# Trainium2, two transformer blocks in one launch: the SiLU of the SSM's first eight channel blocks inside its sixth convolution unit, and the last convolution unit ahead of the SSM input's transposes

## The chip, the cores and the metric

The kernel runs on one core of a Trainium2 chip. The core has TensorE (PE, matrix products and transposes into PSUM), VectorE (DVE), ScalarE (ACT), GpSimd (POOL) and SyncE (SP, which here issues the weight transfers). Each engine runs its own instruction list in order, and the lists are tied together by counting semaphores. The metric is the device time of one launch in microseconds, lower being better.

## The reference, cut to what matters

The launch computes two transformer blocks for 256 tokens of width 1024 in fp32. The change lies in the first block's token mixer, and there in the state-space mixer (SSM):

```python
h = rms_norm(x, pre_mix_norm)
proj = h @ w_in                      # z, xbc, dt_raw, sb_qkv, nsa_q, nsa_kv, nsa_gate, merge_gate
xbc = silu(causal_dwconv(xbc, conv_w, conv_b))   # 2048 channels, 4 taps over time
xs, bm, cm = split(xbc, [1024, 1536])            # xs: SSM input; bm, cm: 4 groups x 128
# ssd_chunked: needs xs with the tokens on rows (times dt), and cm @ bm products
```

Beside the SSM, the same mixer holds a stick-breaking attention ("sb": products of q and k, a log-sigmoid, a reverse cumulative sum, an exponential, products with v) and a sparse attention ("kk", "kv", "vv", "nq"). The rest (gates, feed-forward networks, the second block) is not touched.

## The kernel before

**Units.** All the large weights come as a stream of 128 units of 128 x 2048 fp32 numbers (1 MB). The order is the list `UNITS`: sbq, sbk, sbv (two each, numbers 0 to 5), xbc 0 to 7 (numbers 6 to 13), kk (14), kv (15), vv (16), nq (two), z (four), and so on. SP loads a unit into one of three slots of `w_raw`, as soon as both halves of the unit three places before have been made. fp32 weights are used as a sum of two numbers that PE takes at its faster rate: ACT writes `w_hi` (a rounded copy, function `split` at L1130) and DVE writes `w_lo`, the difference (L1583). ACT may overwrite `w_hi` of a slot only when PE has finished the unit that used it (semaphore `unit_done`). The helper `ahead(name)`, on both engines, makes these halves up to two units beyond the named one, and does nothing when they are made already. For each unit PE multiplies the 256 tokens by the 256 output channels, for two halves of the columns and eight steps of 128 input channels, with three products each (`run_unit`: L466, L468, L469; 48 products), into one of three PSUM banks `pj`. DVE reads that bank out (`channel_major`, L1596), after which the bank is free (`pj_read`).

**Convolution.** A unit xbc i holds channel blocks 2i (even) and 2i+1 (odd). DVE's `conv_out(i)` copies the product to a buffer `xc` (two of them, taken in turn), and then calls `ahead`. ACT's `conv_first(i)` writes the first tap of both blocks (L1223), and one product for POOL (`conv_tap0`, L1231), for which it first waits until POOL has finished the odd block of the unit before (`conv_odd`, one shared buffer). DVE's `conv_taps(i)` adds three taps to the even block (L1599, in unit 7 to both blocks), and POOL's `conv_odd(i)` adds them to the odd block (L403, L406, L400). Then ACT's `silu(q)` treats blocks 4q to 4q+3 in one instruction (L1264). `silu(0)` and `silu(1)` cover the SSM input xs, `silu(2)` and `silu(3)` what becomes bm and cm.

**Order by hand.** Each engine's order is written out. PE: xbc 5, `sb_later(1)` (L636 to L639), xbc 6, a wait for two SiLUs (`xbc_silu` at 2), 16 transposes of the SSM input into PSUM regions S and T (L505), xbc 7, `sb_apply(1)` (L604, L605; needs DVE's `sb_mask(1)`), kk, kv, the "cb" products (L714, L718; need `xbc_silu` at 4), vv, `seg(0)` (L729; needs DVE to have read cb), and so on. ACT: `conv_first(5)`, `sb_exp(1)` (L1253), `silu(0)`, `silu(1)`, `conv_first(6)`, four copies of the transposed input (L1287), `silu(2)`, `conv_first(7)`, `sb_hi(1)` (L1258; needs `sb_apply(1)`), weights of vv, `silu(3)`. DVE: `conv(5)`, `sb_sum(1)`, `sb_mask(1)`, `gate_decay(0)`, `conv(6)`, `conv(7)`, `sb_lo(1)`, the two products xdt, and the read-outs of kk and kv.

ACT holds one set of function tables at a time. Exp and Silu are in different sets; Copy and Identity run with either (the trace shows no load ahead of them).

Of the kernel before, what the change touches and what calls it, by code (L numbers as in the profile page):

```python
# [130 lines left out]
def program(nc, stream, params, consts, cmpw, gains, x_in, out):  # L131
    ctx = ExitStack()
    with ctx:
        sems = {}

        def S(name):

            if name not in sems:
                sems[name] = ctx.enter_context(nc.semaphore(name))
            return sems[name]  # L140
# [29 lines left out]
        def V(kib, *dims):  # L170

            n = int(np.prod(dims))
            o = int(kib * 256)
            ap = area[:, o:o + n]
            if len(dims) == 1:
                return ap
            names = "abcd"[:len(dims)]
            return ap.rearrange(f"p ({' '.join(names)}) -> p {' '.join(names)}",
                                **dict(zip(names[1:], dims[1:])))
# [35 lines left out]
        xbc = V(36, 16, T)  # L215
        xc = [V(52, 2, T), V(54, 2, T)]
# [4 lines left out]
        kk, cm, vv = V(52, 2, T), V(54, 2, T), V(56, 2, T)  # L221
# [77 lines left out]
        def written(ins, region):  # L299
            ins.then_inc(S(f"{region}_written"), 1)  # L300
# [151 lines left out]
        def _(pe):  # L452
            def unit_ready(u):
                pe.wait_ge(S("w_hi_done"), u + 1)
                pe.wait_ge(S("w_lo_done"), u + 1)

            def bank_free(b, n):

                if isinstance(n, int) and n == 0:
                    return  # L460
                pe.wait_ge(S(f"pj_read{b}"), n)
# [11 lines left out]
            def unit_b(slot, b, koff=0, gate=None):  # L473

                for nb in range(2):
                    for k in range(KC):
                        if gate and nb == 0:
                            gate(k)
                        c = k * 256 + nb * P
                        mm = three(pj[b][:, nb * T:(nb + 1) * T], w_hi[:, slot, c:c + P], w_lo[:, slot, c:c + P],  # L480
                                   a_hi[:, koff + k, :], a_lo[:, koff + k, :], k == 0, k == KC - 1)
                mm.then_inc(S("unit_done"), 1)

            def unit_a(slot, b):

                for tb in range(2):
                    for k in range(KC):
                        c = k * 256
                        mm = three(pj[b][:, tb * 256:(tb + 1) * 256], w_hi[:, slot, c:c + 256],
                                   w_lo[:, slot, c:c + 256], a_hi[:, k, tb * P:(tb + 1) * P],  # L490
                                   a_lo[:, k, tb * P:(tb + 1) * P], k == 0, k == KC - 1, weights_left=False)
                mm.then_inc(S("unit_done"), 1)

            def run_unit(name, gate=None):
                u = UIDX[name]
                b, n = BANK[name]
                unit_ready(u)
                bank_free(b, n)
                if name[0] in ("sbv", "vv", "z", "dv", "fv"):
                    unit_a(u % SLOTS, b)  # L500
                else:
                    unit_b(u % SLOTS, b, 8 if name[0] == "wo2" else 0, gate)
# [188 lines left out]
            run_unit(("xbc", 5))  # L691
            sb_later(1)
            run_unit(("xbc", 6))

            pe.wait_ge(S("xbc_silu"), 2)
            claim(pe, "S", "xs")
# [6 lines left out]
                if q == 1:  # L703
                    written(mm, "S")
            written(mm, "T")
            run_unit(("xbc", 7))
            sb_apply(1)
            run_unit(("kk", 0))
            run_unit(("kv", 0))
            claim(pe, "T", "cb")  # L710
            claim(pe, "S", "cb")
# [151 lines left out]
            for n in range(8):  # L863
                name = ("br", n)
# [256 lines left out]
        def _(act):  # L1121
# [70 lines left out]
            for q in range(4):  # L1192
# [4 lines left out]
                for k in (2 * q, 2 * q + 1):  # L1197
                    act.activation(a_hi[:, k, :], pa[:, q, (k % 2) * T:(k % 2 + 1) * T], ACT.Copy,
                                   scale=g_mix1[:, k:k + 1]).then_inc(S("opnd_hi"), 1)
# [14 lines left out]
            for i in range(2):  # L1214
                token_major(("sbv", i), sbv[:, :, i * 256:(i + 1) * 256])

            def conv_first(i):

                ahead(("xbc", i))
                await_value(act, ("xbc", i))  # L1220
                for m in range(2):
                    blk = 2 * i + m
                    act.activation(xbc[:, blk, :], xc[i % 2][:, m, :], ACT.Identity,  # L1223
                                   bias=prm_("cb")[:, blk:blk + 1], scale=prm_("cw")[:, 48 + blk:49 + blk])\
                       .then_inc(S("conv_tap3"), 1)

                if i == 7:
                    return
                if i:
                    act.wait_ge(S("conv_odd"), i)  # L1230
                act.activation(conv_tap0, xc[i % 2][:, 1, :], ACT.Copy, scale=prm_("cw")[:, blk:blk + 1])\  # L1231
                   .then_inc(S("tap3_product"), 1)
# [18 lines left out]
            def sb_exp(p):  # L1251
                await_read(act, "T", f"sb{p}")
                act.activation(sb_w[p], sb_ls[p], ACT.Exp).then_inc(S("sb_exp_ready"), 1)  # L1253
# [7 lines left out]
            def silu(q):  # L1261
                act.wait_ge(S("conv_even"), 2 * (q + 1))
                act.wait_ge(S("conv_odd"), min(2 * (q + 1), 7))
                act.activation(xbc[:, 4 * q:4 * q + 4, :], xbc[:, 4 * q:4 * q + 4, :], ACT.Silu)\  # L1264
                   .then_inc(S("xbc_silu"), 1)
# [10 lines left out]
            conv_first(3)  # L1276
            conv_first(4)
            sb_hi(0)
            conv_first(5)
            sb_exp(1)  # L1280
            silu(0)
            silu(1)
            conv_first(6)
            for q in range(4):
                if q % 2 == 0:
                    await_psum(act, "ST"[q // 2], "xs")
# [4 lines left out]
                else:  # L1291
                    ins.then_inc(S("xs_half"), 1)
            silu(2)
            conv_first(7)
            sb_hi(1)
            ahead(("kk", 0))
            silu(3)
            act.activation(gate, small40[:, :, 16:40], ACT.Tanh, scale=0.5).then_inc(S("gate_tanh"), 1)
            ahead(("kv", 0))
            await_value(act, ("kv", 0))  # L1300
# [275 lines left out]
        def _(dve):  # L1576
# [11 lines left out]
            def ahead(name_or_u):  # L1588
                u = UIDX[name_or_u] if isinstance(name_or_u, tuple) else name_or_u
                while ahead_of[0] <= min(u + 2, N_UNITS - 1):  # L1590
                    split(ahead_of[0])
                    ahead_of[0] += 1
                return u
# [9 lines left out]

            rbc2 = rbc[:, :].unsqueeze(1).to_broadcast([P, 2, T])

            def channel_major(name, dst, scale=None):

                b, _n = BANK[name]
                dve.wait_ge(S("unit_done"), UIDX[name] + 1)
                ins = tt(dst, two(pj[b]), rbc2, ALU.mult) if scale is None \  # L1610
                    else stt(dst, two(pj[b]), scale, rbc2, ALU.mult, ALU.mult)
                ins.then_inc(S(f"pj_read{b}"), 1)
                ahead(name)

            def operand_lo(j, gname, k):
                g = prm_(gname) if j else g_mix1
# [102 lines left out]
            def conv_out(i):  # L1719

                if i >= 2:
                    dve.wait_ge(S("conv_tap3"), 2 * (i - 1))
                    dve.wait_ge(S("conv_odd"), i - 1)
                channel_major(("xbc", i), xc[i % 2])

            def conv_taps(i):

                await_value(dve, ("xbc", i))
                dve.wait_ge(S("conv_tap3"), 2 * i + 1)
                if i == 0:  # L1730
                    dve.wait_ge(S("prm_loaded"), 16)
                for s_ in (1, 2, 3):
                    for m in range(2 if i == 7 else 1):
                        blk = 2 * i + m
                        c = (3 - s_) * 16 + blk
                        if m:
                            dve.wait_ge(S("conv_tap3"), 2 * i + 2)
                        ins = stt(xbc[:, blk, s_:T], xc[i % 2][:, m, 0:T - s_], prm_("cw")[:, c:c + 1],
                                  xbc[:, blk, s_:T], ALU.mult, ALU.add)
                        if s_ < 3:  # L1740
                            V_.did(ins)
                    if s_ == 3:
                        ins.then_inc(S("conv_even"), 1)
                    else:
                        V_.sync()

            def conv(i):
                conv_out(i)
                conv_taps(i)
# [16 lines left out]
            def sb_sum(p):  # L1766
                await_psum(dve, "T", f"sb{p}")
                read(tt(sb_ls[p], sb_ls[p], pt[:, :, 0:384], ALU.add), "T")

            def sb_mask(p):  # L1770
                dve.wait_ge(S("sb_exp_ready"), p + 1)
                tt(outer_blocks(sb_w[p]), outer_blocks(sb_w[p]), sb_diag, ALU.mult).then_inc(S("sb_w_ready"), 1)
# [9 lines left out]
            def gate_decay(g):  # L1782

                tt(gdt, gt.unsqueeze(1).unsqueeze(1).to_broadcast([P, 2, 4, P]),
                   dta[:, :, 4 * g:4 * g + 4].unsqueeze(3).to_broadcast([P, 2, 4, P]), ALU.mult)\
                    .then_inc(S("gdt_ready"), 1)
# [24 lines left out]
            sb_lo(0)  # L1811
            conv(5)
            sb_sum(1)
            sb_mask(1)
            gate_decay(0)
            conv(6)
            conv(7)
            sb_lo(1)

            dve.wait_ge(S("xs_half"), 2)  # L1820
# [553 lines left out]
```

## Time and profile before

| | before |
|---|---|
| median of 3 runs | 909.22 us (903.97 to 910.04) |
| the profiled execution | 908.93 us |
| its span, first to last instruction | 907.1 us |
| outside the span | 1.8 us |
| PE busy | 868.4 us, 96% |
| DVE, ACT, POOL busy | 66%, 51%, 7% |
| mean granted clock of PE | 0.989 |

The profile is of one execution. Spans and durations are in microseconds from the first instruction. "Busy" of PE says that matrix products were in flight, not that they ran at the full rate, so an idle stretch is loss for certain and a busy one may hold loss too. The waits behind an idle stretch are inferred from semaphores, and the one named is the one that came last.

### The profile page before, as it was taken

The numbers are of one execution on the slowest core, as the hardware profiler recorded it, in microseconds if no ns is written. First come the engines' busy times: TensorE is split into PE (matmuls) and PEld (weight loads), VectorE is DVE, ScalarE is ACT, GpSimd is POOL, SyncE is SP. The second block draws the span as 40 slices with busy tenths as digits, with TensorE's granted clock in tenths as the row PEclk, the third lists the DMA queues.
The fourth block names the chain that finished last, engine by engine and source line by source line (L and its number), as shares of the span: only waits on it lengthen the run. The fifth ranks groups of instructions, "written<-read, shape, count | busy, mean of one in ns | idle before, by whom it ended". The sixth has DMA issues, their size and how long they took to land.

```text
span 907.1 us, 15574 instructions
## 1 busy us (share of the span) xinstructions
PE 868.4 (96%) x6246; PEld 805.4 (89%) x6246; DVE 594.3 (66%) x779; ACT 459.5 (51%) x648; POOL 64.7 (7%) x68
## 2 busy tenths in 40 slices
PE   6999799999999999999999999889998999999997
PEld 6999799999988998898999998789885899999995
DVE  4548785626776578678776776876454676555554
ACT  5456743337656444466554555565454463333332
POOL 0026700000000132000000000000000000000000
PEclk9999899999999999999999999999999999999999
DMA  9533352252423345555555555344313446555531
GB/s 341 217 133 140 115 211 94 93 165 79 164 96 137 124 180 197 191 181 186 187 185 185 186 186 186 108 171 141 139 47 116 150 153 222 190 190 186 185 139 47
DMA packets 22168, 143.83 MB, mean 159 GB/s; under 512 B 2928, under 2 KB 3188, under 8 KB 5728
## 3 DMA queue, kind: packets, MB, share of 16 engines
q1 hardware_dynamic: 20304, 138.30, 42.5%
q0 software_dynamic: 1808, 4.73, 1.5%
q8 instruction: 42, 0.69, 0.3%
q14 instruction: 14, 0.11, 0.0%
HBM read 141.96 MB, written 1.84 MB: 159 GB/s over the span
## 4 chain that ended last, share of the span: by engine, by line
PE 82%; DVE 7%; ACT 6%; issue 3%; POOL 2%; DMA 1%; SPq 0%; POOLq 0%; ACTq 0%; DVEq 0%
PE pj L466 16%; PE pj L469 13%; PE pj L468 13%; PE pa L891 6%; PE pa L892 6%; PE pa L893 6%; PE pj L471 2%; PE pj L470 2%; DVE w_lo L1583 2%; PE pa L505 2%; ACT w_hi L1130 1%; PE pj L569 1%; DVE area L1596 1%; ACT area L1374 1%; PE pj L575 1%
## 5 line engine op out<-in xcount | busy, mean ns | idle before, releaser
L1583 DVE TENSOR_TENSOR w_lo<-w_raw,w_hi 128x2048 fp32r<-128x2048 f32 x127 | 294.8, 2323 | 82.1 <-ACT w_hi L1130 81.9
L466 PE MATMUL pj<-a_hi,w_hi 128*128 128x256 f32 x1168 | 335.3, 287 | 0.6 <-issue 0.6
L469 PE MATMUL pj<-a_hi,w_lo 128*128 128x256 f32 x1168 | 332.5, 285 | 0.0
L468 PE MATMUL pj<-a_lo,w_hi 128*128 128x256 f32 x1168 | 332.4, 285 | 0.0
L1130 ACT ACTIVATE w_hi<-w_raw 128x2048 fp32r<-128x2048 f32 x127 | 241.9, 1907 | 56.2 <-PE pa L893 41.4
L466 PEld LDWEIGHTS pj<-a_hi,w_hi 128*128 128x128 f32 x1168 | 226.1, 194 | 5.5 <-issue 4.6
L468 PEld LDWEIGHTS pj<-a_lo,w_hi 128*128 128x128 f32 x1168 | 226.2, 194 | 0.8
L469 PEld LDWEIGHTS pj<-a_hi,w_lo 128*128 128x128 f32 x1168 | 226.0, 193 | 0.0
L891 PE MATMUL pa<-w_hi,a_hi 128*128 128x512 f32 x280 | 109.5, 391 | 4.2 <-issue 4.2
L892 PE MATMUL pa<-w_lo,a_hi 128*128 128x512 f32 x280 | 109.2, 390 | 0.0
L893 PE MATMUL pa<-w_hi,a_lo 128*128 128x512 f32 x280 | 108.9, 389 | 0.0
L1596 DVE TENSOR_TENSOR area<-pj,rbc 128x512 f32<-128x512 f32 x66 | 45.3, 688 | 76.2 <-PE pj L469 75.9
L891 PEld LDWEIGHTS pa<-w_hi,a_hi 128*128 128x128 f32 x280 | 52.7, 188 | 15.1 <-issue 4.8
L893 PEld LDWEIGHTS pa<-w_hi,a_lo 128*128 128x128 f32 x280 | 52.6, 188 | 11.1
L892 PEld LDWEIGHTS pa<-w_lo,a_hi 128*128 128x128 f32 x280 | 52.7, 188 | 9.9
L1599 DVE SCALAR_TENSOR_TENSOR area<-area,prm 128x255 f32<-128x255 f32 (+2 forms) x115 | 52.6, 507 | 2.9 <-ACT area L1223 1.4
L1417 ACT ACTIVATE area<-area,prm 128x256 f32<-128x256 f32 x44 | 24.0, 595 | 54.0 <-DVE area L1596 54.0
L466 PE MATMUL pj<-w_hi,a_hi 128*128 128x256 f32 x176 | 50.5, 287 | 0.0
L471 PE MATMUL pj<-w_hi,a_lo 128*128 128x256 f32 x176 | 49.8, 283 | 0.0
L470 PE MATMUL pj<-w_lo,a_hi 128*128 128x256 f32 x176 | 49.8, 283 | 0.0
L1552 ACT ACTIVATE a_hi<-area 128x512 fp32r<-128x512 f32 x16 | 10.1, 632 | 73.8 <-DVE area L1599 73.8
L1374 ACT ACTIVATE area<-area,tiny 128x128 f32<-128x128 f32 (+1 forms) x64 | 28.4, 444 | 29.4 <-DVE tiny L1953 29.4
(254 smaller groups left out, 1053.2 us busy)
## 6 DMA issues: line engine op xcount, KB each, us to landing
w_raw<-stream SPq DMA_DIRECT2D x127, 1024.0 KB, 4.8
area<-gains POOLq DMA_DIRECT2D x4, 512.0 KB, 4.2
cst<-consts SPq DMA_DIRECT2D x1, 1093.0 KB, 13.4
x_tok<-x_in SPq DMA_DIRECT2D x2, 512.0 KB, 5.0
w_raw<-stream SPq DMA_DIRECT2D x4, 256.0 KB, 6.9
area<-cmpw POOLq DMA_DIRECT2D x1, 1024.0 KB, 5.5
out<-x_tok SPq DMA_DIRECT2D x4, 256.0 KB, 2.0
t_wide<-t_rows POOLq DMA_DIRECT2D x1, 768.0 KB, 13.4
```

Source lines behind the costliest of these rows:

```text
L466: pe.matmul(out_, a[0], a[1], start=first, stop=False)
L468: pe.matmul(out_, wh, al, start=False, stop=False)
L469: return pe.matmul(out_, wl, ah, start=False, stop=last)
L470: pe.matmul(out_, ah, wl, start=False, stop=False)
L471: return pe.matmul(out_, al, wh, start=False, stop=last)
L891: pe.matmul(o_, a_hi[:, chunk + kc, rows], w_hi[:, slot, c:c + 512], start=first, stop=False)
L892: pe.matmul(o_, a_hi[:, chunk + kc, rows], w_lo[:, slot, c:c + 512], start=False, stop=False)
L893: return pe.matmul(o_, a_lo[:, chunk + kc, rows], w_hi[:, slot, c:c + 512], start=False, stop=last)
L1130: act.activation(w_hi[:, slot, :], w_raw[:, slot, :], ACT.Copy).then_inc(S("w_hi_done"), 1)
L1583: dve.tensor_tensor(w_lo[:, slot, :], w_raw[:, slot, :], w_hi[:, slot, :].bitcast(F32), ALU.subtract)\
L1596: return dve.tensor_tensor(o_, a, b, op)
L1599: return dve.scalar_tensor_tensor(out=o_, in0=a, scalar=s_, in1=b, op0=op0, op1=op1)
```

## The change

PE runs xbc 7 straight after xbc 6, then waits for the two SiLUs, then transposes; kk now comes ahead of `sb_apply(1)`. ACT gets an argument `between` for `conv_first`, which runs after the first taps and before the wait for POOL. Inside `conv_first(5)` this makes `w_hi` of kk (unit 14) and runs `silu(0)` and `silu(1)`. Inside `conv_first(6)` it runs `sb_exp(1)` and makes `w_hi` of kv (unit 15). `conv_first(7)` comes ahead of the copies of the transposes, and `silu(3)` follows `silu(2)`. DVE reads xbc 6 out ahead of `gate_decay(0)`, reads xbc 7 out ahead of `sb_mask(1)`, and makes `w_lo` of kv only after that (`split_next`). No work is added or taken away, except that the order of Exp and Silu on ACT is another.

```diff
--- before.py
+++ after.py
@@ -691,6 +691,7 @@
             run_unit(("xbc", 5))
             sb_later(1)
             run_unit(("xbc", 6))
+            run_unit(("xbc", 7))
 
             pe.wait_ge(S("xbc_silu"), 2)
             claim(pe, "S", "xs")
@@ -703,9 +704,8 @@
                 if q == 1:
                     written(mm, "S")
             written(mm, "T")
-            run_unit(("xbc", 7))
+            run_unit(("kk", 0))
             sb_apply(1)
-            run_unit(("kk", 0))
             run_unit(("kv", 0))
             claim(pe, "T", "cb")
             claim(pe, "S", "cb")
@@ -1214,7 +1214,7 @@
             for i in range(2):
                 token_major(("sbv", i), sbv[:, :, i * 256:(i + 1) * 256])
 
-            def conv_first(i):
+            def conv_first(i, between=lambda: None):
 
                 ahead(("xbc", i))
                 await_value(act, ("xbc", i))
@@ -1226,6 +1226,7 @@
 
                 if i == 7:
                     return
+                between()
                 if i:
                     act.wait_ge(S("conv_odd"), i)
                 act.activation(conv_tap0, xc[i % 2][:, 1, :], ACT.Copy, scale=prm_("cw")[:, blk:blk + 1])\
@@ -1276,11 +1277,21 @@
             conv_first(3)
             conv_first(4)
             sb_hi(0)
-            conv_first(5)
-            sb_exp(1)
-            silu(0)
-            silu(1)
-            conv_first(6)
+
+            def early_silu():
+
+                ahead(("xbc", 6))
+                silu(0)
+                silu(1)
+
+            def last_weights():
+
+                sb_exp(1)
+                ahead(("xbc", 7))
+
+            conv_first(5, early_silu)
+            conv_first(6, last_weights)
+            conv_first(7)
             for q in range(4):
                 if q % 2 == 0:
                     await_psum(act, "ST"[q // 2], "xs")
@@ -1291,10 +1302,9 @@
                 else:
                     ins.then_inc(S("xs_half"), 1)
             silu(2)
-            conv_first(7)
+            silu(3)
             sb_hi(1)
             ahead(("kk", 0))
-            silu(3)
             act.activation(gate, small40[:, :, 16:40], ACT.Tanh, scale=0.5).then_inc(S("gate_tanh"), 1)
             ahead(("kv", 0))
             await_value(act, ("kv", 0))
@@ -1603,14 +1613,15 @@
 
             rbc2 = rbc[:, :].unsqueeze(1).to_broadcast([P, 2, T])
 
-            def channel_major(name, dst, scale=None):
+            def channel_major(name, dst, scale=None, split_next=True):
 
                 b, _n = BANK[name]
                 dve.wait_ge(S("unit_done"), UIDX[name] + 1)
                 ins = tt(dst, two(pj[b]), rbc2, ALU.mult) if scale is None \
                     else stt(dst, two(pj[b]), scale, rbc2, ALU.mult, ALU.mult)
                 ins.then_inc(S(f"pj_read{b}"), 1)
-                ahead(name)
+                if split_next:
+                    ahead(name)
 
             def operand_lo(j, gname, k):
                 g = prm_(gname) if j else g_mix1
@@ -1721,7 +1732,7 @@
                 if i >= 2:
                     dve.wait_ge(S("conv_tap3"), 2 * (i - 1))
                     dve.wait_ge(S("conv_odd"), i - 1)
-                channel_major(("xbc", i), xc[i % 2])
+                channel_major(("xbc", i), xc[i % 2], split_next=(i < 7))
 
             def conv_taps(i):
 
@@ -1811,10 +1822,13 @@
             sb_lo(0)
             conv(5)
             sb_sum(1)
+            conv_out(6)
+            gate_decay(0)
+            conv_taps(6)
+            conv_out(7)
             sb_mask(1)
-            gate_decay(0)
-            conv(6)
-            conv(7)
+            ahead(("xbc", 7))
+            conv_taps(7)
             sb_lo(1)
 
             dve.wait_ge(S("xs_half"), 2)
```

## Rows read from the trace of the kernel before

**Rows 1.** The page's section 1 (busy time) and section 6 (weight loads).

```profile
PE 868.4 (96%) x6246; PEld 805.4 (89%) x6246; DVE 594.3 (66%) x779; ACT 459.5 (51%) x648; POOL 64.7 (7%) x68
...
w_raw<-stream SPq DMA_DIRECT2D x127, 1024.0 KB, 4.8
```

**Rows 2.** Timeline of PE: start, length, line, tiles, count, idle before it.

```profile
106.33 3.47 PE L505 MATMUL pa<-cst,area 128*128 128x128 f32 x16 [6.19 <-ACT area L1264]
109.55 0.36 PE L466 MATMUL pj<-a_hi,w_hi 128*128 128x256 f32 x1
...
115.39 0.59 PE L604 MATMUL po<-area 128*128 128x256 f32 x2
...
128.21 1.89 PE L714 MATMUL pa<-area 128*128 128x256 f32 x8
...
130.75 0.36 PE L466 MATMUL pj<-w_hi,a_hi 128*128 128x256 f32 x1
...
224.00 1.91 PE L505 MATMUL pa<-cst,area 128*128 128x128 f32 x16
```

**Rows 3.** Chain of work that ended last, before the transposes: start, length, what.

```profile
99.57 0.70 POOL area L400
...
100.30 0.51 ACT area L1231
```

**Rows 4.** Timeline of ACT: columns as in Rows 2.

```profile
96.56 1.08 ACT L1223 ACTIVATE area<-area,prm 128x256 f32<-128x256 f32 x2
...
102.98 1.28 ACT L1264 ACT_TABLE_LOAD   x1
104.27 2.00 ACT L1264 ACTIVATE area<-area 128x1024 f32<-128x1024 f32 x2
106.18 1.90 ACT L1130 ACTIVATE w_hi<-w_raw 128x2048 fp32r<-128x2048 f32 x1
...
109.37 2.02 ACT L1287 ACTIVATE area<-pa 128x512 f32<-128x512 f32 x4
111.28 1.06 ACT L1264 ACTIVATE area<-area 128x1024 f32<-128x1024 f32 x1
...
117.41 0.64 ACT L1258 ACTIVATE a_hi<-po 128x256 fp32r<-128x256 f32 x2
```

**Rows 5.** Timeline of DVE: columns as in Rows 2.

```profile
96.70 2.29 DVE L1583 TENSOR_TENSOR w_lo<-w_raw,w_hi 128x2048 fp32r<-128x2048 f32 x1 [0.27 <-ACT w_hi L1130]
98.91 2.30 DVE L1599 SCALAR_TENSOR_TENSOR area<-area,prm 128x255 f32<-128x255 f32 x3
101.13 0.94 DVE L1596 TENSOR_TENSOR area<-area,pa 128x768 f32<-128x768 f32 x1
102.99 0.69 DVE L1596 TENSOR_TENSOR area<-area,cst 128x512 f32<-128x512 f32 x1 [0.92 <-ACT area L1253]
103.60 1.66 DVE L1596 TENSOR_TENSOR area<-cst,tiny 128x1024 f32<-128x1024 f32 x1
105.18 0.68 DVE L1596 TENSOR_TENSOR area<-pj,rbc 128x512 f32<-128x512 f32 x1
108.11 2.29 DVE L1583 TENSOR_TENSOR w_lo<-w_raw,w_hi 128x2048 fp32r<-128x2048 f32 x1 [2.25 <-ACT w_hi L1130]
...
118.50 2.69 DVE L1599 SCALAR_TENSOR_TENSOR area<-area,prm 128x255 f32<-128x255 f32 x6
...
121.71 2.35 DVE L1596 TENSOR_TENSOR area<-area,tiny 128x1024 f32<-128x1024 f32 x2
```

**Rows 6.** Timeline of POOL: columns as in Rows 2.

```profile
91.06 2.72 POOL L400 TENSOR_TENSOR area<-area 128x253 f32<-128x253 f32 x1
```

**Rows 7.** Windows: length; busy PE, PEld, DVE, ACT, POOL; then granted clock.

```profile
103.00:104.00 1.00, 0.00 (x0) 0.00 (x0) 1.00 (x2) 1.00 (x1) 0.92 (x2) 0.50 0.41 164
...
110.00:111.00 1.00, 1.00 (x11) 1.00 (x10) 1.00 (x2) 1.00 (x3) 1.00 (x1) 1.00 0.00 0
230.00:231.00 1.00, 1.00 (x7) 1.00 (x7) 1.00 (x1) 1.00 (x2) 0.00 (x0) 0.50 0.08 16
```

## Prediction, written before the changed kernel ran

> **What bounds the kernel now.** I read the page first: PE is busy for 868.4 of 907.1 us, every other engine for at most two thirds [rows 1]. So the kernel ends when PE ends, and an edit is worth the PE time that it frees. Next, the waits of PE and its timeline in the first mixer. Between 60 and 180 us PE stands still once: for 6.19 us, ahead of the 16 transposes at 106.33, until an ACT instruction of L1264, which is SiLU [rows 2]. Xbc 6 was thus over at 106.33 - 6.19 = 100.14. Then the chain of waits, backwards from there: POOL's last add of conv_odd(4) ends at 100.27, ACT's L1231 had waited for it [rows 3], and behind that, on ACT's list, stand sb_exp(1), a table load and the two SiLUs, over at 106.27 [rows 4]. But the SiLUs need none of these. They need the even blocks of units 0 to 3, which DVE had done before its taps of unit 5 at 98.91 [rows 5], and conv_odd(3), over at 91.06 + 2.72 = 93.78 [rows 6]. The stall is one of order on ACT.
>
> Last, the windows, with PE's granted clock. In the idle stretch it is at 0.50, which is the level of 1.2 GHz, and at 110 it is back at 1.00, 2.4 GHz [rows 7]. So the transposes ran at half clock: 3.47 us, where the 16 transposes of the same shape at 224.00 took 1.91 [rows 2]. The stall costs 1.56 us more than its own length.
>
> **What the change takes away.** PE keeps its instructions: from 106.33 to 128.21, where the cb products start, it does transposes, xbc 7, sb_apply(1), kk and kv, without a wait, 21.88 us [rows 2]. In the new order the same work starts at 100.14 with xbc 7. Its weights are there: the `w_lo` ready at 96.70 + 2.29 = 98.99 is the one of unit 13 [rows 5]. Xbc 7 takes 115.39 - 109.55 = 5.84 us [rows 2], so the transposes are due at 105.98. If nothing holds them, PE has not stood still and they run at full clock: 21.88 - 1.56 = 20.32, cb starts at 120.46, and the gain is 6.19 + 1.56 = 7.75 us.
>
> **Does every wait on the way hold?** I follow the three other engines in their new order, with durations of the rows. These overlap their successors by some 0.08 us (98.91 + 2.30 is 101.21, the next starts at 101.13 [rows 5]), so the sums err towards late; hand-overs between engines, below 0.1 us each (106.27 to 106.33), go the other way.
>
> ACT: first taps of unit 5 end at 97.64. `w_hi` of kk, 1.90, to 99.54 (the slot was freed when PE ended xbc 5, which comes before xbc 6 and `sb_later`). Silu load 1.28, two SiLUs 2.00: 102.82 [rows 4]. The transposes want them at 105.98, margin 3.2. Then L1231, 0.51 [rows 3], to 103.33; first taps of unit 6, 1.08, to 104.41; Exp with its load. Those two took from 100.30 + 0.51 = 100.81 to 102.98 [rows 3, 4], 2.17: to 106.58. `w_hi` of kv, 1.90, to 108.48; L1231 to 109.0.
>
> DVE: from sb_sum(1) at 101.13, 0.94; read-out of xbc 6, 0.68; `w_lo` of kk, 2.29: 105.04 (kk starts on PE at 105.98 + 3.22 - 1.56 = 107.64, margin 2.6). gate_decay 1.66, taps of unit 6 2.30, read-out of xbc 7 0.68, to 109.68; sb_mask(1) 0.69, to 110.37 (wanted by sb_apply(1) after kk, at about 113.4, margin 3). `w_lo` of kv 2.29, to 112.66 (kv starts at about 114.7, margin 2). Taps of unit 7, 2.69, to 115.35 [rows 5]. All three margins are those of waits that the edit tightens, since these steps came later or stood behind other work before.
>
> ACT again: first taps of unit 7 after its read-out, 109.68 + 1.08 = 110.76; the four copies 2.02, to 112.78; now the Silu set has to be loaded a second time, 1.28, since Exp came between: this is the one piece of work that the change adds. SiLU 2, 1.06, to 115.12. It lies on ACT beside PE's kk and kv, and SiLU 3 has to wait for DVE (115.35) anyway. SiLU 3 to 116.41, wanted by cb at 120.46, margin 4. sb_hi(1) 0.64, to 117.05, then `w_hi` of vv, 1.90, to 118.95 [rows 4].
>
> DVE again: sb_lo(1), a read-out of 0.68, to 117.73; xdt 2.35, to 120.08; read-out of kk 0.68; `w_lo` of vv 2.29: 123.05 [rows 5]. PE wants vv at 120.46 + (130.75 - 128.21) = 123.00 [rows 2]. **This is the tight spot.** With some ten overlaps of 0.08 off, the weights are ready at 122.2, so I take no wait here and keep 0 to 1 us for the range. What comes next is looser: cb is read by DVE after kv's read-out and unit 17's `w_lo` (126.0) in two products, for which I take at most xdt's 2.35: 128.4, while PE ends vv at 123.0 + 5.84 = 128.84 and only then wants S and T.
>
> POOL: a conv_odd takes 6.5 us (end to end of two of them, 93.78 to 100.27 [rows 3, 6]), so conv_odd(5) ends at 106.8 and conv_odd(6) at 113.3. L1231 of unit 6 wants the first at 108.5, the read-out of xbc 7 at 109.0, SiLU 3 the second at 115.35. The weight transfers are issued earlier than before, as the halves that free their slots are; each takes 4.8 us, and SP is not what PE waits for here.
>
> **Sum.** 907.1 - 7.75 = 899.35 us of span, plus 1.83 outside it (908.93 - 907.1), 901.2. The profiled execution lies 0.3 below the median of 909.22, so by the median 909.22 - 7.75 = **901.5 us**, 0.85% less.
>
> **A rule weighed.** A load of the tables takes 1.28 us, and the SiLU begins 104.27 - 102.98 = 1.29 us after the load did [rows 4]. The Trainium skill, ScalarE: Activation LUTs, "What ACT_TABLE_LOAD costs", states about 2.66 us for every switch of sets, the load and a drain of about 1.38. By the rows a switch is 1.29 and the sum is 901.5; with 1.38 more at each of three switches, the sum would be 904.8 (rival C). I go by the rows.
>
> **Rivals.**
> A. The clock's share doesn't come back in the median. The fall depends on when the stretch begins, and the median may hold executions where the transposes lost less. For it: half-clock stretches of some 3.4 us also stand elsewhere, where nothing waits that long (230 us is in one of three, the others at 212 and 608 [rows 7]). Against it: the clock was down at 103 already, with nothing for PE to do till 106.33, and the transposes took all of 3.47 us [rows 2, 7]. Gain 6.19: 903.0.
> B. PE waits for vv's weights, since the list DVE, SiLU 3, sb_hi, sb_lo, xdt, `w_lo` has no slack. Half the POOL adds in a slow form would do: the same add took 0.69 or 2.72 us [rows 3, 6], and four more slow adds of 2.03 put conv_odd(6) at 121.4, SiLU 3 at 122.5, `w_lo` at 129.1: PE waits 6.1. With one slow add per round, 2 x 2.03, it is 117.4, 118.5 and 125.1, a wait of 2.1: 903.6.
> C. Switches of 1.29 + 1.38 us. The SiLUs are ready at 104.20, still in time; but Exp, the copies and SiLU 2 move on, SiLU 3 ends at 119.63, `w_lo` of vv at 126.3, a wait of 3.3: gain 4.45, 904.8.
> D. More than forecast: the shift of all later work also takes the clock falls at 212 and 230 away. Each halves the clock for some 3.4 us and so costs 1.7 (half of it). Both gone: 898.1. It can go the other way as well, one new fall: 903.2.
> E. Slower. POOL stands between ACT's first taps of unit 6 and all that is queued behind L1231 there: conv_first(7), the copies, both SiLUs, vv's weights. If the rounds of conv_odd doubled to 13 us beside DVE's new order, conv_odd(6) would end at 126.3, `w_lo` of vv at 133.9, PE would wait 10.9 us and lose the clock's 1.56 again: 12.5 - 7.75, 914.0. It decides from a conv_odd(6) that ends after some 122. No round in the trace comes near.
> F. The stall stays, since something else than ACT's order holds the transposes. The regions they claim are free by 102.1 (sb_sum(1)), and the SiLUs have 3 us to spare.
>
> **Chances.** Forecast with up to 1 us of wait at vv, 50%; A, 19%; B, 13%; C, 3%; D's gain, 9%, its loss, 3%; E, 2%; F, 1%. Range: from 898.0 (D, both falls gone) to 905.5 (C, with the scatter of a median of a few runs; the three before span 6 us). About 1% is what a measurement of this kernel can tell from no change; the bound is 900.1. All of D's gain and a good quarter of the forecast's share fall below it by scatter: faster 0.23, same 0.75, slower 0.02.
>
> **What the profile would show.** Right: no idle of PE before L505, which starts near 106 and takes about 1.9 us for 16; granted clock 1.00 from 60 to past 130; L714 near 120.5; SiLUs 0 and 1 over near 102.8; three table loads in ACT between 99 and 115 where two were. Wrong: PE idle ahead of the first matmul of vv, by DVE's L1583 (B, C); conv_odd rounds well over 6.5 us (B, E); a gap over 0.1 between a load and its function (C); half-clock stretches at other places (A, D).

## The result, and the profile after

| | before | after |
|---|---|---|
| median | 909.63 us (903.97 to 914.21, 4 runs) | 899.62 us (897.41 to 904.09, 4 runs) |
| ratio to before, 95% interval | | 0.9898 (0.9874 to 0.9923) |
| the same, second set of runs | 909.17 us (17 runs) | 900.03 us (4 runs), 0.9893 (0.9879 to 0.9908) |
| span of the profiled execution | 907.1 us | 897.7 us |
| mean granted clock of PE in it | 0.989 | 0.993 |

The changed kernel is about 1% faster. The ratios with their intervals aren't the quotients of the medians, which are 0.9890 and 0.9899. The forecast was 901.5 us (a ratio of 0.9915) with a range from 898.0 to 905.5; the measured median is 1.9 us below the forecast and inside the range. The chance that was put on "faster by over 1%" was 0.23; both medians lie just past that bound, and both intervals straddle it.

The page of after, section 1 (busy time by engine), for [rows 1]:

```profile
PE 865.1 (96%) x6246; PEld 801.8 (89%) x6246; DVE 594.6 (66%) x779; ACT 460.8 (51%) x649; POOL 67.4 (8%) x68
```

PE has the same 6246 products and is busy for 3.3 us less; ACT has one instruction more, the added table load. The timeline of PE in the changed kernel (start, length, line, tiles, count, idle before it), for [rows 2]:

```profile
104.47 1.91 PE L505 MATMUL pa<-cst,area 128*128 128x128 f32 x16
...
119.03 1.89 PE L714 MATMUL pa<-area 128*128 128x256 f32 x8
...
121.56 0.36 PE L466 MATMUL pj<-w_hi,a_hi 128*128 128x256 f32 x1
...
127.40 0.60 PE L729 MATMUL pa<-cst,area 128*128 128x256 f32 x2
```

No idle time stands in brackets behind any of these: the 6.19 us ahead of L505 are gone, and the 16 transposes take 1.91 us instead of 3.47. The windows of after show why (length; busy PE, PEld, DVE, ACT, POOL; granted clock), for [rows 7]:

```profile
105.00:106.00 1.00, 1.00 (x12) 1.00 (x10) 0.98 (x2) 1.00 (x2) 0.80 (x2) 1.00 0.51 156
```

PE is busy without a gap here, at a granted clock of 1.00, the level of 2.4 GHz, where it had been at 0.50. The Trainium skill, TensorE: Matmul & The Clock Gate, "Part 1: The HAM clock gate", has it that the slow clock is the default and that activity releases it; at this place the traces agree, 0.50 in and behind the idle stretch, 1.00 without it. But the clock is also at 0.50 from 202 to 206 us in this trace, where PE is busy throughout (1.00 in the windows of 200 and 201 us).

ACT, DVE and POOL in the changed kernel (timelines, same columns), for [rows 4, 5, 6]:

```profile
98.19 1.28 ACT L1265 ACT_TABLE_LOAD   x1
99.48 2.01 ACT L1265 ACTIVATE area<-area 128x1024 f32<-128x1024 f32 x2
...
102.89 1.28 ACT L1254 ACT_TABLE_LOAD   x1
...
110.84 1.28 ACT L1265 ACT_TABLE_LOAD   x1
112.14 1.06 ACT L1265 ACTIVATE area<-area 128x1024 f32<-128x1024 f32 x1
113.98 1.06 ACT L1265 ACTIVATE area<-area 128x1024 f32<-128x1024 f32 x1 [0.79 <-DVE area L1609]
```

```profile
107.68 0.68 DVE L1606 TENSOR_TENSOR area<-area,cst 128x512 f32<-128x512 f32 x1
...
110.48 3.47 DVE L1609 SCALAR_TENSOR_TENSOR area<-area,prm 128x255 f32<-128x255 f32 x6
115.62 0.69 DVE L1606 TENSOR_TENSOR a_lo<-po,a_hi 128x512 fp32r<-128x512 f32 x1 [1.67 <-ACT a_hi L1259]
...
119.10 2.28 DVE L1593 TENSOR_TENSOR w_lo<-w_raw,w_hi 128x2048 fp32r<-128x2048 f32 x1
```

```profile
107.86 3.41 POOL L403 TENSOR_SCALAR area<-area,prm 128x256 f32<-128x256 f32 x1
```

Two SiLUs are over at 101.49, 3 us before PE wants them. The list behind the third table load is the close one: SiLU 3 waits 0.79 us for DVE's taps, DVE waits 1.67 us for ACT's sb_hi(1), and `w_lo` of vv is ready at 119.10 + 2.28 = 121.38, while PE starts vv at 121.56.

**Where the time went.** Two executions of one kernel differ by up to 2 us outside the changed part, so times from the start of the launch can't be compared. I take the starts of PE's marks and their differences. "Local" is from the second `sb_later` (L636, the last step that the change leaves where it was) to the cb products (L714).

| us, from PE's timeline | before | before, 2nd trace | after | after, 2nd trace |
|---|---|---|---|---|
| start to sb_later(1) | 92.48 | 90.62 | 91.21 | 91.58 |
| **local: sb_later(1) to cb** | **35.73** | **36.36** | **27.82** | **27.82** |
| cb to the end | 778.9 | 780.0 | 778.7 | 780.3 |
| span | 907.1 | 907.0 | 897.7 | 899.7 |

The local stretch is 7.9 us shorter than in the first trace of before, 8.5 than in the second. What comes later is the same to within what executions of one kernel differ by. So the gain is where it was looked for, it isn't given back later, and no new wait has taken its place in this stretch. The two first traces differ by 9.4 us in span, since 1.3 us of difference lie ahead of the changed part; in the second traces it is the other way (90.62 and 91.58), so that part is no gain.

### The profile page after: what moved, and what is told of

It reads as the page before. It is cut to its first block, busy times and chain, and to the rows that moved or that the text cites. A ratio compares the mean times of both kernels' runs of the same rounds, so it can differ in the third digit from the quotient of the medians.

```text
span 897.7 us, 15575 instructions
## 1 busy us (share of the span) xinstructions
PE 865.1 (96%) x6246; PEld 801.8 (89%) x6246; DVE 594.6 (66%) x779; ACT 460.8 (51%) x649; POOL 67.4 (8%) x68
## 4 chain that ended last, share of the span: by engine, by line
PE 88%; DVE 6%; ACT 3%; issue 2%; DMA 1%; SPq 0%; ACTq 0%; DVEq 0%
PE pj L466 18%; PE pj L469 15%; PE pj L468 15%; PE pa L891 6%; PE pa L892 6%; PE pa L893 6%; PE pj L471 2%; PE pj L470 2%; PE pa L505 2%; DVE w_lo L1593 2%; PE pj L569 1%; ACT w_hi L1130 1%; PE pj L575 1%; PE pj L571 1%; ACT area L1384 1%
```

## The experiments

All ratios are to the kernel before, timed beside it; the last row is that kernel against itself, so 0.0013 is what a ratio can be off by. The local stretch is read from each trace as above.

| run | ratio (95% interval) | local, us | against before's 35.73 |
|---|---|---|---|
| ACT's part alone | 0.9933 (0.9921 to 0.9945) | 32.23 | -3.50 |
| PE's part alone | 0.9950 (0.9936 to 0.9963) | 32.41 | -3.32 |
| before, its wait filled with products | 0.9967 (0.9951 to 0.9983) | 34.21 | -1.52 |
| after, again | 0.9893 (0.9879 to 0.9908) | 27.82 | -7.91 |
| after, DVE 3 us longer | 0.9922 (0.9896 to 0.9948) | 28.81 | -6.92 |
| the same, vv's `w_lo` first | 0.9921 (0.9903 to 0.9939) | 28.79 | -6.94 |
| after, sb_apply(1) ahead of kk | 0.9928 (0.9910 to 0.9947) | 30.20 | -5.53 |
| after, nsa_scores(0) later | 0.9893 (0.9877 to 0.9909) | 27.82 | -7.91 |
| after, 18 products added | 0.9976 (0.9961 to 0.9992) | 35.58 | -0.15 |
| after, 4 products added | 0.9907 (0.9885 to 0.9928) | 29.55 | -6.18 |
| before, again | 0.9987 (0.9966 to 1.0007) | 36.36 | +0.63 |

### ACT's part alone

```diff
-            conv_first(5)
+            conv_first(5, early_silu)      # ahead(("xbc", 6)), silu(0), silu(1) inside it
             sb_exp(1)
-            silu(0)
-            silu(1)
             conv_first(6)
```

> The kernel before, with ACT's part alone: kk's w_hi and SiLU 0 and 1 inside conv_first(5), then sb_exp(1), then conv_first(6); PE and DVE keep their old order. My theory (each engine's list followed with the durations of the trace): the SiLUs are over 3.4 us earlier (102.8 on the clock of the trace of before, not 106.3), so PE idles about 2.7 us ahead of L505 instead of 6.19 and the transposes run at full clock or lose part of their 1.56; xbc 7 and the rest follow, and kv waits some 0.9 us for its w_lo, since ACT's load of the Silu set and SiLU 2 now stand ahead of it. Gain 3.5 to 4.3 us, ratio 0.9955. Rival (ACT's order was the whole trouble, PE's order is decoration): nearly all of the 7.75, ratio 0.992 or lower. Rival (the early SiLU is of no use without PE's order): no gain.

Timeline of PE in this run:

```profile
100.99 2.38 PE L505 MATMUL pa<-cst,area 128*128 128x128 f32 x16 [2.67 <-ACT area L1265]
```

The wait is 2.67 us, as worked out (2.7). The transposes take 2.38 us, between the 1.91 of full clock and the 3.47 of before. But the granted clock is at 0.50 in the windows of 103 and 104 us, in xbc 7, and cb comes 21.90 us after the start of the transposes, where it came 21.88 after it in the kernel before: the clock's loss is still there in full, only later. The local gain of 3.50 is the shorter wait (6.19 - 2.67 = 3.52) and nothing else. The 0.9 us that was expected ahead of kv doesn't show. By ratio the gain is 6.1 us (0.0067 x 909), more than expected, see below. In the local stretch, moving the SiLUs is worth less than half of the change.

### PE's part alone

```diff
             run_unit(("xbc", 6))
+            run_unit(("xbc", 7))
             pe.wait_ge(S("xbc_silu"), 2)
...
-            run_unit(("xbc", 7))
+            run_unit(("kk", 0))
             sb_apply(1)
-            run_unit(("kk", 0))
```

> The kernel before, with PE's part alone: xbc 7 ahead of the wait for the SiLUs, kk ahead of sb_apply(1); ACT and DVE keep their old order. Theory: xbc 7 covers the time until SiLU 1 (106.3), so the idle ahead of L505 falls from 6.19 to about 0.3 us; but kk's w_hi comes after the SiLUs and its w_lo ends at about 110.4, while PE wants kk at 108.1: a new wait of about 2.3 us ahead of kk, named DVE L1583. Gain about 5 us, ratio 0.9945; together with the first run this would say that the two parts overlap and neither is enough. Rival (the SiLU stays the bound, so PE's order gives nothing by itself): gain 0 to 1. Rival (PE's order is the whole of it): gain 7.75, no wait ahead of kk.

Timeline of PE:

```profile
104.80 1.97 PE L505 MATMUL pa<-cst,area 128*128 128x128 f32 x16 [0.44 <-ACT area L1264]
...
108.98 0.36 PE L466 MATMUL pj<-a_hi,w_hi 128*128 128x256 f32 x1 [2.21 <-issue]
```

The idle ahead of L505 is 0.44 us (0.3 expected), and a new one of 2.21 us stands ahead of kk (2.3 expected). The profile names no releaser for it; DVE's `w_lo` of kk ends right before, in this run's DVE timeline:

```profile
106.59 2.29 DVE L1583 TENSOR_TENSOR w_lo<-w_raw,w_hi 128x2048 fp32r<-128x2048 f32 x1 [2.25 <-ACT w_hi L1130]
```

106.59 + 2.29 = 108.88. What I had left out is the clock: it falls after this wait (0.50 in the windows of 111 and 112 us), which is why the local gain is 3.32 and not 5. The two parts gain 3.50 and 3.32 by themselves and 7.91 together. Each alone leaves an idle of over 2 us, and behind each of these two the clock falls.

### The wait filled with work without use

```diff
             run_unit(("xbc", 6))
+            bank_free(1, 4)
+            keep_warm(1, 13)
             pe.wait_ge(S("xbc_silu"), 2)
```

The 13 products are added and their results are overwritten.

> The kernel before, with 13 products without use (256 columns fp32, about 0.43 us each, 5.6 us in all, into a PSUM bank that xbc 7 starts afresh) in the idle stretch ahead of the wait for the SiLUs. It measures the clock's share alone. Theory: the SiLUs still end at 106.3 and the transposes start there, but the granted clock stays at 1.00 and the 16 take 1.91 us instead of 3.47: what follows is 1.5 to 1.6 us earlier; ratio 0.998, which only the trace can tell. Rival (the transposes were slow for another reason, such as reading xbc right behind the SiLU): 3.47 us again and no gain.

Timeline of PE:

```profile
97.42 5.78 PE L519 MATMUL pj<-cst 128*128 128x256 f32 x26
...
103.77 1.97 PE L505 MATMUL pa<-cst,area 128*128 128x128 f32 x16 [0.57 <-ACT area L1266]
```

The transposes start 13.85 us after sb_later(1), to the hundredth as in before: the SiLUs are as late as ever. But they take 1.97 us, and cb comes 20.36 us later instead of 21.88. The clock's share of the stall is 1.52 us by this run, 1.56 in the forecast. The rival (transposes slow because they read xbc right behind the SiLU) falls. In the second trace of before, the same transposes took 3.67 us and cb came 22.53 us later, so this share is 1.5 to 2.2, according to the execution.

### The changed kernel again, and the kernel before again

> The changed kernel again, on the chip of the three parts. Theory: ratio 0.9915 by the sum (7.75 of 909.2), 0.990 by the first measurement; no wait of PE ahead of L505 at xs, kk, kv, cb or vv.

> The kernel before once more, for a second trace. Expected by both: ratio 1.000; 35.7 us from sb_later(1) to cb as in the first trace; half-clock stretches elsewhere that cost 1.5 us each, at places that need not be the same.

No wait of PE at xs, kk, kv, cb or vv, and the same 27.82 us. The second trace of before:

```profile
104.45 3.67 PE L505 MATMUL pa<-cst,area 128*128 128x128 f32 x16 [6.17 <-ACT area L1264]
```

### Is the tight spot at vv real? DVE made longer

```diff
             conv_out(6)
+            for _n in range(2):
+                V_.did(tt(gdt, gt.unsqueeze(1).unsqueeze(1).to_broadcast([P, 2, 4, P]),
+                          dta[:, :, 0:4].unsqueeze(3).to_broadcast([P, 2, 4, P]), ALU.mult))
+                V_.sync()
             gate_decay(0)
             conv_taps(6)
```

> The changed kernel with two more instructions on DVE like gate_decay(0) (same inputs, same output, each waited for), placed ahead of gate_decay(0): DVE's list is about 3.35 us longer in the middle of the changed part. Theory (the list DVE, SiLU 3, sb_hi, sb_lo, xdt, w_lo of vv has 0.2 us to spare in the trace of after): PE waits about 0.65 us ahead of kv and 2.5 ahead of vv, so seg(0) comes 3.15 us later after sb_later(1) (39.3 us instead of 36.2) and the ratio goes from 0.989 to 0.9925. Rival (other engines give slack, DVE is not near PE's path): under 1 us.

Timeline of PE:

```profile
114.26 0.35 PE L466 MATMUL pj<-a_hi,w_hi 128*128 128x256 f32 x1 [0.75 <-issue]
...
124.31 0.36 PE L466 MATMUL pj<-w_hi,a_hi 128*128 128x256 f32 x1 [1.44 <-issue]
```

The three instructions took 4.65 us where one took 1.65, so DVE was 3.0 us longer, not 3.35. PE waited 0.75 us ahead of kv (expected 0.65) and 1.44 ahead of vv (expected 2.5), and seg(0) came 38.85 us after sb_later(1) instead of 36.19: 2.66 later. 3.0 us more on DVE cost 2.66, so the slack was about 0.3, within what the small changes of other durations allow (DVE's `w_lo` of kv took 2.73 us instead of 2.28, its taps of unit 7 took 2.70 instead of 3.47). The spot is real, and it is about that tight.

```diff
             sb_lo(1)
+            ahead(("kk", 0))        # w_lo of vv ahead of the two xdt products
             dve.wait_ge(S("xs_half"), 2)
```

> The kernel of the run before, with DVE making w_lo of vv ahead of the two xdt products instead of behind kk's read-out. Theory: the wait ahead of vv goes (its w_lo ends near 121.8, wanted at 122.2), the 0.65 ahead of kv stays, and DVE, which still has the same work, is then late with the reading of cb: a wait of about 1.3 us ahead of seg(0). seg(0) 1.95 us later than in the changed kernel, 1.2 earlier than in the run before. Rival (only the one wait at vv counts): seg(0) 0.65 us later. Rival (the order on DVE doesn't matter): 3.15 as in the run before.

Timeline of PE:

```profile
130.42 0.70 PE L729 MATMUL pa<-cst,area 128*128 128x256 f32 x2 [1.46 <-DVE area L1606]
```

The wait ahead of vv is gone and stands ahead of seg(0) instead, 1.46 us. seg(0) comes 38.80 us after sb_later(1), as in the run before. I had expected 0.7 less. DVE's timeline shows what was left out:

```profile
120.58 2.29 DVE L1593 TENSOR_TENSOR w_lo<-w_raw,w_hi 128x2048 fp32r<-128x2048 f32 x1 [1.11 <-ACT w_hi L1130]
```

In its new place `w_lo` of vv has to wait 1.11 us for ACT's `w_hi` of vv, and everything behind it on DVE, the reading of cb included, is late by that. So this run doesn't show what the order alone would give. The changed kernel reads cb out by 126.0 and wants S and T at 127.4: the next spot has 1.4 us.

### One piece undone: sb_apply(1) ahead of kk

```diff
-            run_unit(("kk", 0))
-            sb_apply(1)
+            sb_apply(1)
+            run_unit(("kk", 0))
```

> The changed kernel with one piece undone: PE's sb_apply(1) stands ahead of kk again. Theory: the transposes end at 106.2 on the clock of the trace of after, DVE's sb_mask(1), moved behind the read-out of xbc 7, ends at 108.4, so PE waits 2.1 us ahead of L604, and up to 1.5 more if the granted clock falls. seg(0) 2.1 to 3.6 us later; ratio 0.992. Rival (this piece is for form only, sb_mask is early enough): no change.

Timeline of PE:

```profile
109.64 0.67 PE L604 MATMUL po<-area 128*128 128x256 f32 x2 [2.14 <-DVE area L1606]
```

2.14 us of waiting, 2.38 us longer locally, ratio 0.9928 instead of 0.9893. The swap of kk and sb_apply(1), one line of the diff, carries a good quarter of the gain. It covers what the new order of DVE costs: sb_mask(1) starts at 108.81 in this run, behind gate_decay(0), the taps of unit 6 and the read-out of xbc 7. Exp, which sb_mask also needs, had ended at 106.16 and was not what it waited for. The granted clock stays at 1.00 behind this wait: 2.14 us of waiting cost no clock here, where 2.21 us ahead of kk did in the run with PE's part alone. So not every such wait has the clock's share on top.

### The next wait of PE

The waits of PE, 60 to 240 us, in the second trace of the changed kernel begin with (line, who is waited for: total, times, longest):

```profile
PE pa L593 <- DVE a_lo L1609: 1.8, 1, 1.8
```

```diff
-            nsa_scores(0)
             run_unit(("gm", 3))
+            nsa_scores(0)
```

> The changed kernel, with PE's nsa_scores(0) moved behind the unit gm 3, to cover the wait of 1.8 us ahead of L593 that stands in the traces of both kernels in the same way. Theory: the wait goes, and the first round of probabilities, which ACT and DVE start only after their work for gm 3 anyway, is some 0.3 us late: gain 1.5 us over the changed kernel, ratio 0.9875. Rival: the time comes back as a wait ahead of the first round_turn, no gain. Rival: slower, since DVE's nsa_soft(0) now holds up the read-out of gm 3 and its bank.

The wait isn't in this run's list any more. From the two transposes of `cmp_e` (L505, at 208.85 in after) to the first product at L569 behind them (367.62) it is 157.48 us instead of 158.77: 1.29 us gained in the trace. Part of the 1.75 us came back as the rival said, since the waits for DVE's L1980 grew from 0.94 to 1.42 us in all. The ratio is that of the changed kernel (0.9893 in both); 1.3 us is less than these intervals can tell. I don't claim it as faster.

### Why do the timed runs gain more than the trace?

Both parts and the filled kernel gain more by ratio than in their local stretch: 6.1 against 3.5, 4.5 against 3.3, 3.0 against 1.5, and the changed kernel 9.3 to 9.7 against 7.9. (The medians alone differ by 5.3, 3.9, 2.8 and 10.0 or 9.1 us; the kernel before against itself gives 1.2 us by ratio, 0.5 by median.) Two more runs ask whether the place of the later work does it. The edit in both is a number of products without use between xbc 7 and the wait for the SiLUs, 18 or 4.

> The changed kernel with 18 products without use (7.78 us by the spacing of 0.432 seen in the filled stretch before) between xbc 7 and the wait for the SiLUs: all later work stands where it stands in the kernel before, within 0.1 us, but without PE's idle stretch. It asks where the 1.5 us come from by which the medians gain more (9.4 to 9.7 us) than the stretch from sb_later(1) to cb does in the traces (7.9). Theory P (place): the half-clock stretches elsewhere depend on when the later work begins, so they are those of the kernel before; ratio 1.000. Theory C (the count of half-clock stretches elsewhere isn't tied to the place of the later work): the gain of the median stays, the fill costs its length, ratio 0.9895 + 7.78 / 909.2 = 0.998.

> The same with 4 products, 1.73 us: later work 6.2 us earlier than in the kernel before. Theory C: the time is that of the changed kernel plus 1.73, ratio 0.9914, same median clock of 0.993 to 0.991. Theory P: off from that by 1.5 us or more, with a granted clock to match.

With 18, the later work stands where it stands in the kernel before, and yet the ratio is 0.9976: the gain of the changed kernel less the length of the fill, as theory C says (0.998). With 4 it is 0.9907 (theory C: 0.9914). This speaks against the place as the cause, though not by much: 0.9976 has an interval of 0.9961 to 0.9992, which leaves out 1.000, but the kernel before, timed again in the same set, came out at 0.9987 (0.9966 to 1.0007). The granted clocks of the timed runs agree: 0.987 in 17 of the 23 runs of before of this set, but 0.993 or more in 8 of the 12 runs with 18 products. The stall itself (clock at half for some 7 us) makes up about 0.004 of that, the rest is about one half-clock stretch of 3.4 us fewer elsewhere in the launch. What such a stretch costs can be read from the marks: from the product at L762 to the first at L792 it is 23.01 us in the trace of before, 24.50 with ACT's part alone and 26.04 in the second trace of before, with the same instructions; the windows show no half clock there in the first, 3.4 us of it in the second and 6.8 in the third. That is 1.5 us for each 3.4.

The profiles don't show that there are fewer of them. Outside the stall and the last 10 us of the launch, the windows have three stretches of 3.4 us (or their sum) in the first trace of before and four in the second, and likewise three and four in the two of after.

So of the 9.5 us or so, 7.9 to 8.5 are the stall with its transposes. The rest, about 1 us, is no larger than the 1.2 us by which the kernel before differs from itself; one half-clock stretch fewer would pay for it. Whether the kernel with the stall really has more of them, as the clocks of the timed runs say and the four profiles don't, and if so why, stays open.

## Why the prediction was right, point by point

**The chain.** The SiLUs were held by order alone, and PE by the SiLUs: right. With ACT's part alone the wait fell to 2.67 us, with PE's part alone to 0.44.

**The lists.** On the clock of the trace of before (1.27 us added to the one of after, whose sb_later(1) comes so much earlier), the working compares like this:

| | forecast | measured |
|---|---|---|
| SiLU 0 and 1 over | 102.82 | 102.76 |
| `w_lo` of kk | 105.04 | 104.90 |
| sb_mask(1) over | 110.37 | 109.63 |
| `w_lo` of kv | 112.66 | 111.83 |
| SiLU 3 over | 116.41 | 116.31 |
| `w_lo` of vv / vv started | 123.05 / 123.00 | 122.65 / 122.83 |
| conv_odd(5), conv_odd(6) over | 106.8, 113.3 | 106.96, 114.02 |
| cb started | 120.46 | 120.30 |

(Measured, from rows that aren't shown above: `w_lo` of kk 101.31 + 2.32, `w_lo` of kv 108.28 + 2.28, the ends of conv_odd 104.20 + 1.49 and 112.06 + 0.69; 1.27 is added to each.) Every step is within 0.9 us, and the tight spot was named and is tight by 0.2. Following three engines with durations of rows was enough. The sums for ACT, DVE and PE erred to the late side, as said; those for POOL to the early one, by 0.2 and 0.7 us. In the list behind SiLU 3 a longer piece than forecast (DVE's taps, 3.47 us for 2.69) made up for the earlier start, so that the closeness there is in part luck.

**The size of the local gain.** 7.75 forecast, 7.91 measured. The 0.16 is what the end of xbc 6 would give: the idle of 6.19 is counted from the modelled end of a 0.28 us product, but the next product could have started 0.12 us after that one's start.

**The table switch.** The three loads of after take 1.28 us each, and the function starts 1.29 to 1.30 us after the load did. The load itself starts 0.02 us after the `w_hi` ahead of it ends (96.26 + 1.91 = 98.17, 98.19). The Trainium skill, ScalarE: Activation LUTs, "What ACT_TABLE_LOAD costs", states about 2.66 us for a switch with its drain; no trace here shows the drain, and the measurement decides. Rival C is out.

**The term that was mis-sized** is the clock's. The forecast took 1.56 us from one trace; the second trace of before has 2.2. And it took the half-clock stretches elsewhere as chance of either sign (rival D, a gain at 9%, a loss at 3%), at 1.7 us each, half of 3.4; they cost 1.5, and the clocks of the timed runs point to about one fewer. The two together have the size of the 1.9 us between 901.5 and 899.6, but no run splits that difference, and a good part of it can be the scatter of two medians of four runs. In hindsight the chance of faster by over 1%, 0.23, was too low: both medians came out at that bound.

**The rivals.** A (the clock's share doesn't come back) falls by the filled run, 1.52 us, and by the 1.91 us of the transposes in after. B and E (POOL) had a grain: one POOL instruction did take 3.41 us instead of 0.93, but the round ended at 114.02 on the clock of before, 1.2 us ahead of DVE's taps, and SiLU 3 waited for DVE, not for it. F fell with the first trace. The half-clock stretches at 212 and 608 us that A and D lean on don't stand in [rows 7], which show only the one at 230; the trace of before has all three (211 to 216, 228 to 233, 607 to 612).

## What to carry to other kernels

When the bound engine waits, look at what the releasing instruction itself needs, and at what merely stands ahead of it on its engine: here the SiLU had its inputs at 93.8, and its engine's list let it go at 103.0. Moving it and filling the hole from the other side were each worth under half in the changed stretch, and the follow-up swap (kk ahead of sb_apply) was worth 2.4 us; such an edit has to be worked through on every engine's list. Price an idle stretch of TensorE with the slow products behind it: 1.5 us and more here on top of 6.2, about 1.5 on top of 2.67 and of 2.21, and nothing on top of 2.14 in one trace.

## What the runs showed of the hardware

POOL and DVE instructions that run side by side are at times much longer than alone. The one-input POOL instruction L403 takes 0.93 us in the median of its 14, and 3.41 at 107.86 in the trace of after, while DVE ran sb_mask and a `w_lo` (two inputs from SBUF each); the other traces with this order have 3.42 and 3.43 at the same place. DVE's six taps of unit 7 took 3.47 us beside POOL's last adds, and 2.69 in the kernel before, where POOL had ended; with DVE 3 us longer, POOL had ended too, and the taps took 2.70. The Trainium skill, GPSIMD Engine Reference, "Specifications", says that POOL shares its SBUF interfaces with VectorE, with contention when VectorE has two SBUF inputs. The traces fit that, with 2.5 us for one instruction as the highest price, but don't prove it: no run was made for it, and the L403 at 101.02 took 0.93 us though a `w_lo` ran beside it from 101.31.

Half the clock for 3.4 us costs about 1.5 us of launch time, and how often that happens differs between executions of one kernel. Of 52 timed runs of the kernel before (two of the sets), the 2 with a granted clock of 0.993 took 903.5 us in the mean, the 8 with 0.989 took 908.5, the 37 with 0.987 took 909.5 and the one with 0.980 took 915.0. So these stretches are likely most of the spread of the changed kernel too, from 897.41 us (0.997) to 904.09 (0.987).
